# A hybrid encoder step on one core: the first norm weight loaded as one row and spread by TensorE, with extra products of the identity in TensorE's first waits

## What is computed

```python
def _rmsnorm(x, g):
    y = x * lax.rsqrt(jnp.mean(x * x, axis=-1, keepdims=True) + EPS)
    return y * g

z = _rmsnorm(x, g_attn) @ w_in          # q | k | v | forget logits | pool input u | memory query | gates
kv = _rmsnorm(mem, g_mem) @ w_mkv
# three branches (forgetting attention, trailing means, cross attention), gated and merged:
h = x + (sum_b sigmoid(gate_b) * W_b(branch_b)) @ w_out
y = h + relu(_rmsnorm(h, g_mlp) @ w_up) ** 2 @ w_down
```

## Time and profile before

| what | value |
| --- | --- |
| median of 3 runs | 1990.22 us (1988.85 to 1991.16) |
| span of the profiled execution, first to last instruction | 1988.2 us |
| median less span | 2.0 us |
| TensorE busy | 98% of the span |
| VectorE, ScalarE, GpSimd busy | 50%, 32%, 10% |

### The profile page before, as it was taken

One profiled execution on the slowest core, in us unless ns is written; L12 is line 12 of the kernel. 1 busy time (PEld: TensorE's weight loads), 2 busy tenths in 40 slices (PEclk: granted clock), 3 DMA queues, 4 the chain that ended last, 5 costly groups with the idle time before them and its releaser, 6 DMA issues.

```text
span 1988.2 us, 28685 instructions
## 1 busy us (share of the span) xinstructions
PE 1949.2 (98%) x11595; PEld 1906.9 (96%) x11595; DVE 988.6 (50%) x1889; ACT 645.5 (32%) x1234; POOL 195.8 (10%) x280
## 2 busy tenths in 40 slices
PE   7999999999999999999999999999999999999998
PEld 7999999999989999999999999999999999999997
DVE  6675545454556466553333465444444444444444
ACT  6444434353545443442223332111111111111124
POOL 0003324250611122000000000000000000000000
PEclk9999999999999999999999999999999999999999
DMA  6441312213166533453233211110202020111212
GB/s 183 116 131 49 91 46 63 82 38 106 34 228 195 190 112 99 147 161 105 84 90 91 79 43 38 32 54 27 59 28 59 27 58 28 53 32 54 70 37 85
DMA packets 209959, 164.23 MB, mean 83 GB/s; under 512 B 15518, under 2 KB 186526, under 8 KB 209829
## 3 DMA queue, kind: packets, MB, share of 16 engines
q1 hardware_dynamic: 209829, 162.41, 26.9%
HBM read 132.86 MB, written 29.51 MB: 82 GB/s over the span
## 4 chain that ended last, share of the span: by engine, by line
PE 87%; DVE 4%; issue 3%; ACT 2%; POOL 2%; DMA 1%; SPq 0%; DVEq 0%; POOLq 0%; ACTq 0%
PE ps L1243 72%; PE ps L1227 3%; PE ps L1081 2%; PE ps L1069 2%; PE ps L1002 1%; PE ps L917 1%; PE ps L1012 1%; PE ps L1036 1%; POOL fox_p L866 1%; PE ps L1151 1%; PE ps L989 1%; ACT w_hi L444 0%; DVE prod L2123 0%; ACT fox_pt_hi L1397 0%; PE ps L1138 0%
## 5 line engine op out<-in xcount | busy, mean ns | idle before, releaser
L1243 PE MATMUL ps<-act_hi,w_hi 128*128 128x384 f32 x1800 | 611.5, 340 | 1.7 <-DVE fox_q_lo L2083 0.9
L1243 PE MATMUL ps<-act_hi,w_lo 128*128 128x384 f32 x1800 | 602.6, 335 | 0.0
L1243 PE MATMUL ps<-act_lo,w_hi 128*128 128x384 f32 x1800 | 602.1, 335 | 0.0
L1243 PEld LDWEIGHTS ps<-act_hi,w_hi 128*128 128x128 f32 x1800 | 338.1, 188 | 3.4 <-issue 2.7
L1243 PEld LDWEIGHTS ps<-act_lo,w_hi 128*128 128x128 f32 x1800 | 338.3, 188 | 0.7
L1243 PEld LDWEIGHTS ps<-act_hi,w_lo 128*128 128x128 f32 x1800 | 337.8, 188 | 0.0
L444 ACT ACTIVATE w_hi<-w_raw 128x512 fp32r<-128x512 f32 (+1 forms) x172 | 147.0, 855 | 303.8 <-PE ps L1243 300.8
L462 DVE TENSOR_TENSOR w_lo<-w_raw,w_hi 128x512 fp32r<-128x512 f32 (+1 forms) x172 | 168.1, 978 | 132.6 <-ACT w_hi L444 132.5
L1243 PE MATMUL ps<-ff_hi,w_hi 128*128 128x384 f32 x672 | 227.0, 338 | 0.0
L1243 PE MATMUL ps<-ff_lo,w_hi 128*128 128x384 f32 x672 | 227.0, 338 | 0.0
L1243 PE MATMUL ps<-ff_hi,w_lo 128*128 128x384 f32 x672 | 227.0, 338 | 0.0
(11 more groups left out here) (311 smaller groups left out, 2827.7 us busy)
## 6 DMA issues: line engine op xcount, KB each, us to landing
w_raw<-in_w_in_dram SPq DMA_DIRECT2D x44, 512.0 KB, 4.3
w_raw<-in_w_up_dram SPq DMA_DIRECT2D x32, 512.0 KB, 4.1
w_raw<-in_w_down_dram SPq DMA_DIRECT2D x56, 256.0 KB, 2.7
merged<-prod SPq DMA_DIRECT2D x48, 192.0 KB, 1.9
prev<-merged SPq DMA_DIRECT2D x48, 192.0 KB, 4.2
foxs_kraw<-in_cache_fox_k_dram SPq DMA_DIRECT2D x8, 1024.0 KB, 5.6
foxs_vraw<-in_cache_fox_v_dram SPq DMA_DIRECT2D x8, 1024.0 KB, 5.9
out_dram<-fin_y SPq DMA_DIRECT2D x18, 256.0 KB, 2.0
```

The source lines that it names most:

```text
L1243: last = nc.tensor.matmul(bank(b)[:, 0:width], W[k][a][:, t, :], moving[z][:, t, j * width:(j + 1) * width], start=(t == 0 and n == 0), st ...
```

## The change

- SP loads `g_attn` as a single row into `g_row` on one partition (4 KB instead of 512 KB).
- GpSimd makes a row of 128 ones, `one_row`, between the identity and the clearing of `W[0][0]`; the counts that others wait for move up by one.
- TensorE no longer starts with tile 0's transposes. It makes four products of the identity with itself into PSUM bank 4, waits for the row, spreads it over 128 partitions by two products of contraction length 1 (128 x 512 each, float32) into banks 6 and 7, and makes six more products of the identity. Behind the transposes of tiles 0 to 4 it makes three more each. Nobody reads what the products of the identity write.
- VectorE, behind its first memset, waits for the spread and copies 128 x 1024 elements out of PSUM to `g_x`; `scaled(0)` waits for that copy and no longer for a DMA.

```diff
+        g_row = tensor("g_row", [1, D], R_AT + 40960)
+        one_row = tensor("one_row", [1, P], C_AT + 1024)
...
-        g_in = group("g", "attn", "mem", "fin")
+        g_in = group("g", "attn", "spread", "kept", "mem", "fin")
...
         def forget_hi(act):
-            act.wait_ge(consts_made, 2)
+            act.wait_ge(consts_made, 3)
...
             load_tile(0)
-            sp.dma_start(g_x[:], g_attn.rearrange("l d -> (l d)").partition_broadcast(P)).then_inc(g_in["attn"], 16)
+            sp.dma_start(g_row[:], g_attn).then_inc(g_in["attn"], 16)
...
             nc.gpsimd.affine_select(out=ident[:], ...).then_inc(consts_made, 1)
+            nc.gpsimd.memset(one_row[:], 1.0).then_inc(consts_made, 1)
             nc.gpsimd.memset(W[0][0][:].bitcast(F32), 0.0).then_inc(consts_made, 1)
...
-            pe.wait_ge(consts_made, 1)
+            def awake(n):
+                for _ in range(n):
+                    nc.tensor.matmul(ps[:, 4, 0:P], ident[:], ident[:], start=True, stop=True)
+
+            pe.wait_ge(consts_made, 2)
+            awake(4)
+            pe.wait_ge(g_in["attn"], 16)
+            for c in range(2):
+                last = nc.tensor.matmul(ps[:, 6 + c, :], one_row[:], g_row[:, c * D // 2:(c + 1) * D // 2],
+                                        start=True, stop=True)
+            last.then_inc(g_in["spread"], 1)
+            awake(6)
             for t in range(NT + MT):
                 pe.wait_ge(xn["scaled"], 2 * (t + 1))
...
                 last.then_inc(xn["turned"], 1)
+                if t < 5:
+                    awake(3)
...
                 if t == 0:
-                    dve.wait_ge(g_in["attn"], 16)
+                    dve.wait_ge(g_in["kept"], 1)
...
             nc.vector.memset(u_t[0][:], 0.0).then_inc(po["clear"], 1)
+            dve.wait_ge(g_in["spread"], 1)
+            nc.vector.tensor_copy(g_x[:], ps[:, 6:8, :].rearrange("p a c -> p (a c)")).then_inc(g_in["kept"], 1)
...
-            dve.wait_ge(consts_made, 3)
+            dve.wait_ge(consts_made, 4)
```

## The result

The changed kernel takes 1994.84 us (median of 9 runs, 1991.63 to 1996.79) against 1990.22 for the kernel before beside it (9 runs, 1988.85 to 1991.48): ratio 1.0021, 95% interval 1.0012 to 1.0030. Run again on another occasion it took 1993.93 (11 runs) against 1990.16: ratio 1.0022, interval 1.0013 to 1.0031. So it is slower by 3.8 to 4.6 us, 0.2%, and not within a microsecond of before as forecast.

A forecast was written before the change was run, and what follows sets the result against it. VectorE reaching tile 1 was taken to bound the opening, with TensorE busy 98% overall. Tile 1's scaling +1.0 us and -0.16 at tile 9 gave +0.84 on 1990.22, so 1991.1 us, range 1988.0 to 1993.8.

The forecast's parts named there:

- the bias was the bound at tile 9: At tile 9, ScalarE's wait for `f_b` (until 31.71 us before) moves with VectorE, limiting what a fast TensorE gives back.
- The row's landing: Load of the single weight row, behind tile 0's load: taken to land at 4.5 us, ends 3.7 and 4.8.
- the four products: Identity products on TensorE ahead of the spread: end at 3.7 us, before the row lands, so cost nothing.
- the copy: VectorE's copy of 1024 columns from PSUM to `g_x`: 1.23 us, on the path to tile 1's scaling.
- The spread: Two single-row products on TensorE: 1.71 us fast or 3.41 slow, plus 0.2; end taken as 7.75 us.
- if the clock rises 4.5 us after TensorE's first work: In the opening, TensorE's clock would rise at 6.5 us and the spread end at 7.4, not 8.1.
- Tile 0's transposes: On TensorE behind tile 0's scaling: no delay was charged for them.
- The 0.16 us: At tile 9's transposes, a fast TensorE wins back 37.13 - 36.97 = 0.16 us before the bias bounds.
- What the change touches ends with the eleven tiles: The change's effect ends at about 43 us; from tile 9 to 59 us everything moves as one.
- the pile-up: Rival: clock stays low, added products bound TensorE at 3.04 us a tile; +4.9 us, 1995.1, chance 0.12.
- The clock rises early and covers the spread: Rival: spread takes 1.71 us, opening gains 0.3 to 0.8 us and the 0.16; 1987.6 to 1989.7 us, chance 0.13.
- The third rival: Clock up only at 26 us, nothing piles up, delay stays whole: +1.0 to +1.35, 1991.2 to 1991.6 us, chance 0.08.

The follow-up runs named there:

- awake_only: Kernel before, DMA of `g_x` kept, with ten identity products ahead of tile 0 and three behind each of tiles 0 to 4: 1992.49 us, ratio 1.0016.
- row_only: Changed kernel without any product of the identity, so the row, its spread and the copy alone: 1992.61 us, ratio 1.0012 to the kernel before.
- after_head: Changed kernel with its head identity products made as three wide ones and none behind the tiles: 1991.96 us, ratio 1.0014 to the kernel before.
- before_again: The kernel before, unchanged, run once more for its profile: 1989.96 us, ratio 1.0001.

## Why the prediction was wrong

The forecast was 1991.1 us, 1988.0 to 1993.8, and 0.87 for no difference; measured were 1994.84 and 1993.93.

What bounds the opening was read rightly. VectorE's order from tile 1 on carried the delay, the bias was the bound at tile 9 (33.91 us against the 32.7 expected, moved with VectorE as said; 0.7 us early once the load was moved), and TensorE at the full clock bought nothing (`awake_only`: 0.2 us).

The row's landing (4.5 expected, 4.65), the four products (3.7; they ended at 3.84) and the copy (1.23; 1.22) held. **The spread** was a middle of 3.25 us between clock up and clock down, and it measured 3.77: it ran at the low clock from end to end. The step of the opening that failed is "if the clock rises 4.5 us after TensorE's first work". In the five executions with the single-row products ahead of tile 0 it rose at 12.7 to 14.5 us (in the changed kernel at 14.5, though TensorE had worked without a gap since 4.65); with the identity's products alone it rose at 4.6 to 7.0. Whether the single-row products themselves hold the rise back was not tested apart. Tile 1 was scaled 1.55 us late and not 1.0.

**Tile 0's transposes** were costed at nothing, as I had the clock up by then. At the low clock they held ScalarE's copy, its statistics of tile 3 and so VectorE: +0.65 on top of the 1.55. The lines for it were in my trace of before: transposes that ended at 9.92 and their copy at 10.69, so 0.77 us of slack. The transposes came 3.2 us late, as tile 0's scaling did (9.81 for 6.55), and used that up, so the copy came 2.46 us late. It is a queue that I did not follow: what stands behind a waiting instruction on ScalarE.

**The 0.16 us** given back were not there. I compared 37.13, where the chain's piece begins at the modelled end of the piece before it, with the start of the same transposes in the timeline (36.97); starts against starts, tile 9 moved by 2.17 us.

So the opening is +2.2 for +0.84: right in sign and place, short by 1.4 us. That alone would have given 1992.4 us, inside the range, and it is close to what `row_only` (+2.4) and `after_head` (+2.2) measured.

**The step that made it wrong** is "What the change touches ends with the eleven tiles", with "if anything after 60 us hung on the opening, which I found no row for". An added instruction shifts all that follow it in TensorE's stream, and with them the 16 KB blocks in which the stream is fetched. A line for it was there: queue 8 with 92 transfers, in the profile's page of before. I gave no price to 108 instructions beyond their own time. It was 1.6 to 2.4 us, of which the collision near 88 us accounts for 0.7 to 1.1 in the two profiles; the rest lies near 560 and 920 us, and which wait it goes through stays open.

Of the rivals, the pile-up was forecast at 1995.1 us and the time came close to that, but the mechanism is not the one: TensorE was never the bound behind tile 1, its transposes from tile 2 on ran at the full clock, and `awake_only` piled up nothing. "The clock rises early and covers the spread" fell as well. The third rival, that TensorE gives nothing back and the delay stays whole, describes the opening best, with 2.2 us in place of its 1.0 to 1.35, though the clock was up at 14.5 us and not at 26.

The Trainium skill's sentence on transposes ("TensorE: Matmul & The Clock Gate", "Part 4: PE-mode transpose"), that the full clock does not engage for them, is contradicted here: in `before_again` the clock rose at 17.5 us with nothing but transposes ahead, and in `row_only`, with transposes and the single-row products, at 14.2.

## What to carry to other kernels

In a kernel where one engine executes tens of thousands of instructions, adding a few dozen at its head can cost more time than they take: try the same number of idle increments in the same wait, and compare with that. Before a load is made cheaper, ask what comes in its place on the engines that wait next; here 1.5 us of transfer, hidden behind another transfer, was traded for 5 us of spread and copy that nothing hid. And a slack found at one wait must be followed through the next engine's queue as well.

## What I had not expected of the hardware

- A 512 KB load that takes 4.0 to 4.3 us took 5.1 to 5.5 with an instruction block of 16 KB beginning well inside it, in three of three traces.
- 32 increments of a semaphore that nobody reads, in a wait, made a 1990 us kernel 2.4 us slower (1.0013, interval 1.0004 to 1.0022).
- The clock's first rise, where no identity products stood alone ahead of tile 0, moved between 12.7 and 26.3 us, in one program between two executions (17.5 and 26.3), without a measurable effect on the time here.
- A product of contraction length 1 was no cheaper than a full one: 3.75 to 3.78 us for four records of 512 columns at the low clock, where an estimate from line 1183, scaled to that clock and to 512 columns, gives 3.6.
